# Last two keys of the first projection as split products, x turned in two places, squares summed on VectorE

## The reference

```
mod   = silu(c) @ ada_w + ada_b                      # six vectors of 1024
a     = rmsnorm(x, g_pre) * (1 + mod[1]) + mod[0]
b, cg, v = split(a @ sc_w_in, 3)                     # 1024 x 3072
y     = (b * conv3(cg * v, sc_conv)) @ sc_w_out
h     = x + mod[2] * rmsnorm(y, g_post)
h     = h + mod[5] * rmsnorm(relu(modulate(rmsnorm(h)) @ w_in)^2 @ w_out)
```

## Time and profile before

| | us |
|---|---|
| median of three runs | 751.59 |
| lowest, highest | 751.36, 751.73 |
| the profiled execution | 751.48 |
| its span | 749.8 |
| TensorE busy | 743.3 |
| VectorE busy | 553.0 |
| ScalarE busy | 364.0 |

### The profile page before, as it was taken

How to read it: one execution, slowest core, us unless ns; L and a number is a source line. 1 busy time by engine, 2 the same in 40 slices (tenths; PEclk the granted TensorE clock), 3 DMA queues, 4 the chain that set the end, 5 groups by cost and what they waited for, 6 DMA issues and landing times.

```text
span 749.8 us, 13272 instructions
## 1 busy us (share of the span) xinstructions
PE 743.3 (99%) x5364; PEld 692.3 (92%) x5364; DVE 553.0 (74%) x795; ACT 364.0 (49%) x453; POOL 12.2 (2%) x29
## 2 busy tenths in 40 slices
PE   8999999999999999999999999999999999999998
PEld 8889955999998888899979999999999999999998
DVE  4767998856556833589899967859879988887441
ACT  4125332754554334496555356585556655554330
POOL 0000000000000000020000011000000000000000
PEclk9999999999999999999999999999999999999999
DMA  9999998365566967536445342337553555443640
GB/s 313 349 368 329 360 375 304 124 226 183 168 181 215 350 207 226 194 127 226 169 168 174 109 169 99 130 129 261 179 215 132 206 194 198 151 145 122 203 139 29
DMA packets 53455, 152.70 MB, mean 204 GB/s; under 512 B 2784, under 2 KB 33888, under 8 KB 43168
## 3 DMA queue, kind: packets, MB, share of 16 engines
q1 hardware_dynamic: 52576, 149.43, 57.5%
q0 software_dynamic: 544, 1.84, 0.7%
q10 hardware_dynamic: 288, 0.76, 0.3%
HBM read 150.97 MB, written 1.05 MB: 203 GB/s over the span
## 4 chain that ended last, share of the span: by engine, by line
PE 85%; DVE 7%; ACT 3%; DMA 3%; issue 1%; SPq 1%; ACTq 0%; DVEq 0%
PE ps L1467 19%; PE ps L1466 19%; PE ps L1465 19%; PE ps L1627 4%; PE ps L1626 4%; PE ps L1625 4%; PE ps L1672 4%; PE ps L1547 4%; DMA raw<-in_ada 3%; DVE w_lo L902 3%; DVE cacc L1239 2%; ACT w_hi L538 1%; PE ps L1796 1%; PE ps L1794 1%; PE ps L1795 1%
## 5 line engine op out<-in xcount | busy, mean ns | idle before, releaser
L902 DVE TENSOR_TENSOR w_lo<-raw,w_hi 128x2048 fp32r<-128x2048 f32 (+2 forms) x116 | 246.0, 2123 | 84.6 <-ACT w_hi L538 84.6
L1465 PE MATMUL ps<-a_hi,w_hi 128*128 128x256 f32 x1024 | 290.4, 284 | 0.0
L1467 PE MATMUL ps<-a_hi,w_lo 128*128 128x256 f32 x1024 | 289.5, 283 | 0.0
L1466 PE MATMUL ps<-a_lo,w_hi 128*128 128x256 f32 x1024 | 288.1, 281 | 0.0
L538 ACT ACTIVATE w_hi<-raw 128x2048 fp32r<-128x2048 f32 (+2 forms) x116 | 205.8, 1778 | 98.5 <-PE ps L1627 48.4
L1465 PEld LDWEIGHTS ps<-a_hi,w_hi 128*128 128x128 f32 x1024 | 193.2, 189 | 1.3 <-issue 0.7
L1466 PEld LDWEIGHTS ps<-a_lo,w_hi 128*128 128x128 f32 x1024 | 193.5, 189 | 0.6 <-issue 0.5
L1467 PEld LDWEIGHTS ps<-a_hi,w_lo 128*128 128x128 f32 x1024 | 191.8, 187 | 0.0
L1465 PE MATMUL ps<-up_hi,w_hi 128*128 128x256 f32 x192 | 54.6, 284 | 0.0
L1467 PE MATMUL ps<-up_hi,w_lo 128*128 128x256 f32 x192 | 54.3, 283 | 0.0
L1466 PE MATMUL ps<-up_lo,w_hi 128*128 128x256 f32 x192 | 53.8, 280 | 0.0
(11 more groups left out here) (274 smaller groups left out, 934.2 us busy)
## 6 DMA issues: line engine op xcount, KB each, us to landing
raw<-in_w_z_in SPq DMA_DIRECT2D x26, 1024.0 KB, 4.8
raw<-in_w_up SPq DMA_DIRECT2D x22, 1024.0 KB, 4.8
raw<-in_w_mlp_in SPq DMA_DIRECT2D x16, 1024.0 KB, 4.9
raw<-in_w_mlp_out SPq DMA_DIRECT2D x16, 1024.0 KB, 5.7
raw<-in_w_down SPq DMA_DIRECT2D x16, 704.0 KB, 4.0
raw<-in_ada SPq DMA_DIRECT2D x16, 512.0 KB, 9.0
raw<-in_ada_half SPq DMA_DIRECT2D x8, 1024.0 KB, 7.9
raw<-in_ada SPq DMA_DIRECT2D x8, 1024.0 KB, 5.8
```

The source lines that it names most:

```text
L902: e.tensor_tensor(w_lo[:, slot, 0:words], raw[:, unit_slot, 0:words], w_hi[:, slot, 0:words].bitcast(f32), SUB).then_inc(raw_used, 1)
L1465: e.matmul(dst, w_hi[:, slot, cols], hi, start=start, stop=False, skip_group_check=skip)
L1466: e.matmul(dst, w_hi[:, slot, cols], lo, start=False, stop=False, skip_group_check=skip)
L1467: return e.matmul(dst, w_lo[:, slot, cols], hi, start=False, stop=stop, skip_group_check=skip)
```

## The change

Four things change.

First, steps 6 and 7 are no longer plain fp32. ScalarE rounds the last pair of keys into the room of pair 0 (`key_high`, in two halves, behind the modulation of tiles 5 and 6), VectorE subtracts (`key_low`), and TensorE multiplies in split products (`by_split_key`). Their activations need low parts before the step, so the low parts of tiles 6 and 7 are made one by one and ahead of those of tiles 0 to 5. Since split keys now fill w_hi's and w_lo's slots 1 and 2, `w_used` is raised by three at the end of step 7 only.

Second, the second half of x is turned four matmuls at a time, in steps 1 and 3, into bank 6, and copied out by ScalarE ahead of the modulation of tiles 2 and 4; the six fillers of step 1 go.

Third, VectorE adds the squares of both engines, and TensorE folds four tiles instead of eight; four fillers follow. ScalarE takes silu behind both its squares.

Fourth, VectorE reads column 3 between the two halves of part 4, column 4 behind part 5, column 5 behind part 6, and the fold of column 6 comes after the second group of step 5.

```
@@ -346,6 +349,10 @@
     return keyed[pair % 2], pair // 2 * KEY_WORDS
+def key_split(t, lo, hi):
+
+    return t[:, :, :].rearrange("p s f -> p (s f)")[:, UNIT + lo:UNIT + hi]
+
 def pcol(name, i=0, n=1):
@@ -620,11 +627,11 @@
     e.activation(x_tok[:, 0, 0:512], flat(x[:, 0:2, :]), ACT.Square).then_inc(x_sq, 1)
+    e.wait_ge(x_landed[1], 16)
+    e.activation(x_tok[:, 0, 512:1024], flat(x[:, 4:6, :]), ACT.Square).then_inc(x_sq, 1)
     e.wait_ge(const_set, 1)
     e.wait_ge(par_in, 16)
     e.activation(silu_c[:, :], pcol("c", 0, 8), ACT.Silu).then_inc(c_ready, 1)
-    e.wait_ge(x_landed[1], 16)
-    e.activation(x_tok[:, 0, 512:1024], flat(x[:, 4:6, :]), ACT.Square).then_inc(x_sq, 1)
     e.preload_act_table_set("natural_log_exp_and_others")
@@ -632,6 +639,13 @@
     e.activation(x_tok[:, :, 0:512], ps[:, 0:2, :], ACT.Copy).then_inc(x_tok_in, 1)
+    def key_high(h):
+
+        e.wait_ge(key_in[3][h], 16)
+        e.wait_ge(keys_free, 1)
+        lo, hi = h * KEY_WORDS // 2, (h + 1) * KEY_WORDS // 2
+        e.activation(key_split(w_hi, lo, hi), key_slot(3)[0][:, KEY_WORDS + lo:KEY_WORDS + hi], ACT.Copy).then_inc(key_hi, 1)
+
     def modulated(t):
@@ -644,12 +658,19 @@
         e.activation(a_hi[:, t, :], y[:, t, :], ACT.Copy).then_inc(act_hi, 1)
+    def x_by_token(pair):
+
+        e.wait_ge(tile_turned, pair)
+        e.activation(x_tok[:, :, 2 * pair * P:(2 * pair + 2) * P], ps[:, 6, :].rearrange("p (c i) -> p c i", c=2), ACT.Copy)\
+         .then_inc(x_tok_in, 1)
+
     for t in range(DT):
+        if t in (2, 4):
+            x_by_token(1 + t // 2)
         modulated(t)
         a_high(t)
-        if t == 0:
-            e.wait_ge(tile_turned, 2)
-            e.activation(x_tok[:, :, 512:1024], ps[:, 2:4, :], ACT.Copy).then_inc(x_tok_in, 1)
+        if t in (5, 6):
+            key_high(t - 5)
         if t == 6:
@@ -917,12 +938,19 @@
         ada_part(src[:, D:2 * D], silu_c[:, k + 1:k + 2], acc).then_inc(raw_used, 1)
-    def pair_sum(q, v):
+    def key_low(h):
+
+        e.wait_ge(key_hi, h + 1)
+        lo, hi = h * KEY_WORDS // 2, (h + 1) * KEY_WORDS // 2
+        e.tensor_tensor(key_split(w_lo, lo, hi), key_slot(3)[0][:, KEY_WORDS + lo:KEY_WORDS + hi],
+                        key_split(w_hi, lo, hi).bitcast(f32), SUB).then_inc(key_lo, 1)
+
+    def pair_sum(q, v, halves=(0, 1)):
         u = 2 * q + v
         acc = pair_acc[:, q % 2, v, :]
         src = raw[:, u % RAW_SLOTS, :].rearrange("p (i j f) -> p i j f", i=2, j=4)
-        for i in range(2):
+        for i in halves:
             e.wait_ge(part_in[u][i], 16)
@@ -1056,10 +1084,15 @@
     two = flat(x[:, 2:4, :])
-    e.tensor_tensor(x_tok[:, 1, 0:512], two, two, MUL).then_inc(x_stat_in, 1)
+    first = ch.mark(e.tensor_tensor(x_tok[:, 1, 0:512], two, two, MUL))
     e.wait_ge(x_landed[1], 16)
     two = flat(x[:, 6:8, :])
-    e.tensor_tensor(x_tok[:, 1, 512:1024], two, two, MUL).then_inc(x_stat_in, 1)
+    ch.mark(e.tensor_tensor(x_tok[:, 1, 512:1024], two, two, MUL))
+    for h in range(2):
+        cols = slice(h * 512, (h + 1) * 512)
+        e.wait_ge(x_sq, h + 1)
+        ch.wait(first + h)
+        e.tensor_tensor(x_tok[:, 0, cols], x_tok[:, 0, cols], x_tok[:, 1, cols], ADD).then_inc(x_stat_in, 1)
     e.wait_ge(c_ready, 1)
@@ -1075,14 +1108,23 @@
     pair_sum(1, 1)
-    for t in range(2, DT):
-        if t == DT - 1:
-            a_low(0, 6)
-        columns(t)
-        if t < DT - 2:
-            pair_sum(t // 2 + 1, t % 2)
+    columns(2)
+    pair_sum(2, 0, (0,))
+    columns(3)
+    pair_sum(2, 0, (1,))
+    pair_sum(2, 1)
+    columns(4)
+    pair_sum(3, 0)
+    columns(5)
+    pair_sum(3, 1)
+    columns(6)
+    key_low(0)
+    a_low(6, 7)
+    key_low(1)
+    columns(7)
+    a_low(7, 8)
+    a_low(0, 6)
     low(0, 0, WORDS["sc_in"])
-    a_low(6, DT)
     low(1, 1, WORDS["sc_in"])
@@ -1498,22 +1540,23 @@
     mm.then_inc(tile_turned, 1)
-    e.wait_ge(x_sq, 1)
     for h in range(2):
         e.wait_ge(x_stat_in, h + 1)
-        if h:
-            e.wait_ge(x_sq, 2)
-        for engine in range(2):
-            for i in range(2):
-                at = h * 512 + i * T
-                mm = e.matmul(ps[:, 6, 0:T], ones[:, :], x_tok[:, engine, at:at + T],
-                              start=h + engine + i == 0, stop=h + engine + i == 3)
+        for i in range(2):
+            mm = e.matmul(ps[:, 6, 0:T], ones[:, :], x_tok[:, 0, h * 512 + i * T:h * 512 + (i + 1) * T],
+                          start=h == 0 and i == 0, stop=h == 1 and i == 1)
     mm.then_inc(x_stat, 1)
-    e.wait_ge(x_landed[1], 16)
-    for c in range(2):
-        for i in range(4):
-            mm = e.matmul(ps[:, 2 + c, i * P:(i + 1) * P], x[:, 4 + i, c * P:(c + 1) * P], ident[:, :], start=True, stop=True)
-    mm.then_inc(tile_turned, 1)
+    keep_busy(4)
+
+    def turn_x(pair):
+
+        if pair == 3:
+            e.wait_ge(x_tok_in, 2)
+        for i in range(2):
+            for c in range(2):
+                at = c * T + i * P
+                mm = e.matmul(ps[:, 6, at:at + P], x[:, 2 * pair + i, c * P:(c + 1) * P], ident[:, :], start=True, stop=True)
+        mm.then_inc(tile_turned, 1)
     def tile_columns(t):
@@ -1544,7 +1587,18 @@
             opens = k == 0 and (n == 0 or n == 2 and h == 0)
-            mm = e.matmul(half(bank, h), lhs, y[:, k, :], start=opens, stop=k == DT - 1, skip_group_check=True)
+            mm = e.matmul(half(bank, h), lhs, y[:, k, :], start=opens, stop=False, skip_group_check=True)
+        return mm
+
+    def by_split_key(k, grp):
+
+        for n in range(3):
+            at = (3 * grp + n) * 256 + k % 2 * P
+            bank, h = (SC_BANKS[grp][0], n) if n < 2 else SC_BANKS[grp][1:]
+            dst = half(bank, h)
+            e.matmul(dst, key_split(w_hi, at, at + P), a_hi[:, k, :], start=False, stop=False, skip_group_check=True)
+            e.matmul(dst, key_split(w_hi, at, at + P), a_lo[:, k, :], start=False, stop=False, skip_group_check=True)
+            mm = e.matmul(dst, key_split(w_lo, at, at + P), a_hi[:, k, :], start=False, stop=k == DT - 1, skip_group_check=True)
         return mm
@@ -1555,30 +1609,38 @@
     e.wait_ge(x_tok_in, 1)
-    for k in range(DT):
+    for k in range(6):
         e.wait_ge(a_ready, k + 1)
         for grp in range(4):
             if k % 2 == 0 and grp % 2 == 0:
                 e.wait_ge(key_in[k // 2][grp // 2], 16)
-            if k == 0 and grp == 2:
-                e.wait_ge(x_tok_in, 2)
             mm = by_key(k, grp)
-            if k == DT - 1 and grp < 3:
-                mm.then_inc(sc_done, 1)
-            if grp == 2 and k == 1:
+            if grp == 2 and k in (1, 3):
                 e.wait_ge(cols_ready, 2)
-                keep_busy(6, 6)
-            if grp == 2 and 0 < k < DT - 1:
+                turn_x(2 + k // 2)
+            if grp == (1 if k == 5 else 2) and k > 0:
                 tile_columns(k + 1)
         if k == 3:
-            mm.then_inc(w_used, 1)
-    mm.then_inc(w_used, 2)
+            mm.then_inc(keys_free, 1)
+    for k in (6, 7):
+        e.wait_ge(act_lo, k - 5)
+        for grp in range(4):
+            if k == 6 and grp % 2 == 0:
+                e.wait_ge(key_lo, grp // 2 + 1)
+            mm = by_split_key(k, grp)
+            if k == 7 and grp < 3:
+                mm.then_inc(sc_done, 1)
+            if k == 6 and grp == 0:
+                tile_columns(7)
+    mm.then_inc(w_used, 3)
     g0 = FIRST["sc_in"]
     e.wait_ge(act_lo, DT)
     for b in range(8):
         grp = 4 + b // 2
+        if b == 0:
+            e.wait_ge(x_tok_in, 3)
         if b % 2 == 0 and grp > 4:
...
```

More of the change, by code:

```diff
@@ L254, in build_program @@
         key_in = [[sem(f"key_in{q}_{h}") for h in range(2)] for q in range(4)]
+        keys_free = sem("keys_free")
+        key_hi = sem("key_hi")
+        key_lo = sem("key_lo")
         sc_w_in = [sem(f"sc_w_in{j}") for j in range(4)]
@@ L1488, in mod_sums, with keep_busy @@
                     mod_sum(vector, acc, i, bank)
-            def keep_busy(n, bank=5):
+            def keep_busy(n):
                 for _ in range(n):
-                    e.matmul(ps[:, bank, 0:P], ident[:, :], ones[:, :], start=True, stop=True)
+                    e.matmul(ps[:, 5, 0:P], ident[:, :], ones[:, :], start=True, stop=True)
             e.wait_ge(const_set, 3)
```

## The result

The changed kernel takes **753.08 us** (median of 19 runs, 752.81 to 757.18) against 751.61 for the kernel before beside it: a ratio of 1.0026, 95% interval 1.0020 to 1.0033. That is 1.5 us slower where +0.4 was forecast, and just outside the range of 750.0 to 753.0. The profiled execution took 753.08, its span is 751.4 against 749.8.

A forecast was written before the change was run, and what follows sets the result against it. TensorE, nearly always busy, was taken as the bound. Steps -1.4, block 1 and its gate product +1.68 and +0.42, old slack -0.35 gave +0.35, about +0.4, on 751.48: 751.9 us, range 750.0 to 753.0.

The forecast's parts named there:

- the part on block 2: Block 1's high part, subtraction and gate product fall behind step 7; TensorE waits 1.7 us, block 2 starts 0.4 later.
- Steps 6 and 7 at 9.0 to 9.3 us: Split fp32r products make these two steps take 9.0 us plus none to 0.3, where they took 10.94.
- the term for the start of step 6: Step 6 starts at 53.0 instead of 52.64, 0.4 us later (0.1 to 1.7), behind VectorE's subtraction and low part.
- The sum of part 3: VectorE's sum in the opening ends at 26.55 as before; the fold comes then and step 2 at 28.3.
- the fold of step 3: TensorE's fold in the opening, due at 32.3, nine matmuls after step 2's start; step 3 starts at 34.0.
- the way from step 4 to step 6: Stretch of the opening steps from 41.1 to 53.0, 11.9 us.
- the wait of 0.4: TensorE reaches the fold of column 6 at 49.5 and waits 0.4 us for part 7, summed by about 49.9.
- The 0.9 us gained at step 2: In the opening, step 2 starts at 28.3 instead of 29.26, 0.9 us earlier.
- From there all rows later by a constant: After block 2, every later row shifts by a constant 0.2 to 0.7 us.
- (a): No wait at block 2, so the whole 1.4 us stays: 750.1 us, at most 749.6; chance 0.18.
- (b): Block 5's load, issued about 65.7 instead of 61.89, lands late and stalls VectorE 3.1 us: 753.0 us; chance 0.12.
- (c): TensorE's clock falls in the new pauses of 0.4 to 1.7 us, adding some 3.6: 755.5 us; chance 0.04.

The follow-up runs named there:

- experiment 1: Changed kernel with the first half of the split keys in other room, so slot 1 is free behind step 3: 751.33 us against 751.83 for the kernel before.
- experiment 2: Kernel before with only the two early slot-count raises put together behind step 7, nothing split: 753.57 us against 751.83.
- Experiment 3: Changed kernel with steps 6 and 7 again plain fp32 and the old slot release, opening edits kept: 752.58 us against 751.83 for the kernel before.
- experiment 7: Changed kernel with x turned as before, all ahead of the steps, six fillers in step 1: 752.90 us against 751.66 for the kernel before.
- experiment 5: Kernel before with steps 6 and 7 split, first half of split keys in other room, slot 1 released behind step 3: 751.27 us against 751.71.
- experiment 4: Kernel before with the split of steps 6 and 7 alone, slots released together behind step 7, old opening: 753.12 us against 751.83.
- experiment 9: experiment 5 with column 6 folded one group earlier and step 6 begun on high-part products: 750.52 us against 751.66 for the kernel before.

## Why the prediction was off

**The mechanism was right, in every step of the part on block 2.** ScalarE's high part 0.26 after the first product of the stage: 0.25. The gate product and block 2's subtraction behind block 1's: 66.07 - 62.2 = 3.87 us after the stage's start, measured 3.78. 6.51 us from there to the end of the second product: 73.32 - 66.83 = 6.49. From stage to block 2, 10.4 forecast, 10.33 measured, with a wait of 1.53 for 1.7. Experiments 1 and 2 show that the late slot is its cause, at 1.75 and 1.74 us. Steps 6 and 7 at 9.0 to 9.3 us: 9.18.

**The step that failed is the term for the start of step 6**, "0.4 later (0.1 to 1.7)". It was 1.23 later. With it the stage began 0.53 early instead of 1.4, and the sum, redone with measured terms, is -0.53 + 1.69 = +1.16 instead of +0.35. Of these 0.87 us (53.87 for 53.0) about 0.77 are already there at step 4 (41.87 for 41.1), and small errors with one sign make them. The text's own bounds for this term reached 1.7, and it says that a later end of step 7 makes the whole as much later: carried on, its upper bound gives 751.9 + 1.3 = 753.2. The stated range did not carry it on. The errors:

- The sum of part 3 was to end at 26.55, as before. It began at 23.02, behind a landing that the trace of before did not show as a wait, and the fold came at 27.08: 0.53 late. This fold also wanders from program to program, between 26.75 and 27.83 with the changed opening, and between 27.51 and 28.77 with the old one, where TensorE's own work sets it.
- So the fold of step 3 came at 32.87, not 32.3, while the first half of part 4 was summed by 32.48. VectorE could not go on to the second half, because the read of column 3 stands ahead of it in the queue: it idled 1.01 us, where the forecast had VectorE read the column at about 32.9. Part 5 ended at 39.97, not 39.4.
- A fold that TensorE has waited for takes longer to be read. From its start to VectorE's read there are 0.64 us (27.08 to 27.72; likewise 40.03 to 40.67), against 0.54 in the row the forecast used, and to the step 1.84 instead of 1.75. (The fold of column 3 at 32.87, for which TensorE did not wait, took 0.61, to 33.48.)
- Right, on the other hand, was the way from step 4 to step 6: 11.9 us forecast, 12.00 measured. The low part of tile 6 at 0.42 was right as well (53.40, 0.42 us), and it ended at 53.82, just as TensorE came free.

Experiment 3 gives the opening's share a price of its own: 0.75 us (1.0 by the spans) for edits that had been costed at next to nothing. Half lies before step 4 (with the scatter told there), half behind it, at the earlier fold of column 6; the second half was in the forecast (the wait of 0.4 and what follows), the first was not. In the program before, TensorE's own work sets step 4 (no wait after 35.52); in the changed one the chain of experiment 7 does, and it is 14.79 us from the fold of step 2 to step 4 (27.08 to 41.87) where the forecast had 14.55 and an earlier start. The 0.9 us gained at step 2 by the forecast (0.34 measured) are spent before step 4 either way.

**A second term was missing**: the 0.46 us standstill of VectorE at 477 us, +0.4 on the spans. "From there all rows later by a constant" was true up to 471 us and then not. Without it the spans would be some 1.2 us apart, so the time, by estimate 752.7, would have stood inside the range by luck, with a start of step 6 that was just as wrong. Nothing in the trace of before points to it.

**Rivals.** (a), no wait at block 2, is false here, but experiment 1 shows what it would have been worth: 751.33, not 750.1, since the stage began only 0.53 early and the standstill at 477 us is in that kernel too. (b), the load of block 5: its issue did move, from 61.89 to 66.61 (the second of the two in the row below), but ScalarE's copies run on at one in 3.4 us (block 4 at 71.00, block 5 at 74.38) with no wait for a load. So the load landed within 7.8 us, where the rival needed 9.9, and (b) is false. SyncE:

```profile
61.42 5.57 SPq L440 DMA_DIRECT2D raw<-in_w_sc_in  x2
```

(c), the clock: the granted clock is 1.00 in a window of 2 us that holds 1.38 of the 1.53 us of the pause at block 2 (TensorE busy 0.62 of the window), and the products behind it have the pitch of 0.12 (73.60, 73.72, 73.84):

```profile
72.00:74.00 2.00, 0.62 (x5) 0.62 (x6) 1.93 (x5) 0.78 (x2) 0.00 (x0) 1.00 0.99 398
```

So (c) is false for pauses of this length. The Trainium skill (TensorE: Matmul & The Clock Gate, "HAM oscillation — how this bites in real kernels") tells of a clock halved after waits for data between groups of matmuls, in an example whose waits are all longer than any pause here. No run here has such a wait, so that is neither borne out nor refuted.

**The sum of the parts, as measured:** the opening +0.75 (experiment 3); the split with its own room -0.44 (experiment 5); the late slot +1.74 (experiment 2). Together +2.05, where the whole change is +1.47; the middle term is within the noise of its run. Most of the overlap is at step 6, which is 1.11 late in experiment 3, 1.41 late in experiment 4 and only 1.23, not 2.52, in the changed kernel: the split alone waits 1.11 us there for the low part of tile 6; in the changed kernel the fold of column 6 stands earlier, and that low part is ready when TensorE comes. Against it stands the standstill at 477 us, some 0.4 us, which is in the whole and in none of these three parts.

## What to carry to other kernels

A buffer borrowed for a new step costs by the time at which its slot comes free, so list the next three users of that slot on every engine before the saving is counted: here 1.76 us of cheaper matmuls were lost to a later start and to a release that came behind step 7 instead of step 3, and 16 KB a partition of other room took the release's 1.7 us back. Where a forecast joins several handoffs between engines in series, each taken from the best row, their small errors add with one sign; a wait that begins at a DMA landing deserves a margin of the landings' own spread (here the fold behind such a landing started over a spread of 1.1 us in the programs with the changed opening). And a small fold that stands one group earlier can be worth more than the cheaper matmuls seem to be: with the split and its own room, moving the fold of column 6 ahead gave the larger part of the 0.75 us of experiment 9, while the same move without the split (experiment 3) only added a wait.

## What the runs showed of the hardware

- Four dependent additions on VectorE are followed after 0.10 us by an addition that needs their result in one program, and after 0.46 us in another, with the same instructions around it (475.19 to 477.32 against 473.95 to 475.72). It is 0.46 in all four programs that have it, at the same place; each was profiled once. Five more instructions ahead of it, in the kernel before, don't bring it about. No cause was found.
- A column fold that ends a wait of TensorE reaches VectorE 0.64 us after its start (27.08 to 27.72, 40.03 to 40.67), one in a running stream 0.54 (45.82 to 46.36), but 0.61 in one place (32.87 to 33.48).
- A pause of TensorE of 1.53 us left the granted clock at 1.00 and the pitch of the matmuls at 0.12 us.
